# First attention of a fused two-layer kernel: its steps run beside the A projections and half of the output projection

## The chip, the cores and the metric

The kernel runs on one core of one Trainium2 chip. Its metric is the device time of one execution in microseconds (us), compared as the median over several runs.

## The reference, cut to what matters

Two different transformer layers follow each other on a sequence of 512 tokens with 1024 features, all in float32. The change touches the first layer, up to its MLP:

```python
# 512 tokens = 4 tiles of 128 queries; all scores are causal
h = rmsnorm(x, g_pre_mix)
proj = h @ w_in              # q_a k_a v_a | q_i k_i w_i | q_d k_d v_d
# A: 8 heads of 64; each query keeps its 128 best keys, chosen by the indexer
#    sum_h w_i[h] * relu(q_i[h] . k_i)
o_a = softmax(q_a k_a^T / 8, only the kept keys) @ v_a
# D: 4 heads, two maps of 64 each, values 128 wide
o_d = (softmax(q1 k1^T / 8) - lam * softmax(q2 k2^T / 8)) @ v_d
o_d = rmsnorm(o_d) * (1 - lam_init)
x = x + rmsnorm(concat(o_a, o_d) @ w_out, g_post_mix)
x = x + rmsnorm(relu(rmsnorm(x) @ w_up)**2 @ w_down, g_post_mlp)
# then the second layer: windowed attention + mLSTM + a mixture of 32 experts
```

## The kernel before

Every engine has a program of its own, written out by hand in the order in which it runs, and counts semaphores to wait for the others. Tokens lie in 4 tiles of 128 (NT). Eight PSUM banks are handed round.

The projections of the first layer are the list G1 of 30 groups. A group is 8 matmuls in the source, 16 on the engine, of 128x512 with 128 rows. A "rope" group is followed by 4 ScalarE copies of 32 partitions that swap halves (the swaps, L1458) and by 3 VectorE operations (the rope, L1869 to L1871). A "val" group is followed by one ScalarE copy. The order is: 4 groups of q_i, one of k_i, 4 of q_d with a small one for w_i, 4 of k_d, 4 of v_d, and then the A projections, 4 each of q_a, k_a and v_a. Their weights come in chunks through a ring of two slots: a chunk is loaded when the one two before it has been used. Between the groups TensorE runs the indexer's maps (idx_part, L845), three behind each of 8 groups, and VectorE runs the selection of the kept keys (take_steps, 48 passes of MAX8 and MATCH_REPLACE8, L1851 and L1852).

Then comes the attention, alone. It has 48 units: for each query tile i, whose rows are w = 128(i+1) wide, 4 "diff" units (one head of D, two maps) and 8 "topk" units (one head of A, one map), a diff and a topk unit by turns and the last four topk units behind. A unit is: its scores on TensorE (L854), the mask with the row maximum on VectorE (L1927, L1934), the exponential on ScalarE (L1486), for a diff unit the difference of the two maps on VectorE (L1941 to L1945), transposes of 128x128 blocks on TensorE (L865), a copy of them on ScalarE (L1494), and the product with the values on TensorE (L877). TensorE runs the scores of unit a, the transposes of unit a-2 and the values of unit a-3; the scores take turns in 4 banks.

Behind it TensorE turns the mixed output (T_MIX, L786), runs the output projection in 8 groups of the same size (L901, one for each token tile and half of the columns), and turns the normed result (T_MLP) for the MLP, whose up projection starts at L926. Much later the second layer runs a windowed attention in steps of two units (L1134, L1142, L1155), most of them with a dense group (L1065) beside them.

## Time and profile before

| | |
|---|---|
| median of 3 runs | 1961.93 us (1958.96 to 1975.52) |
| profiled execution | 1976.24 us, span 1974.3 us |
| TensorE busy | 1872.6 us, 95% of the span |
| VectorE, ScalarE busy | 780.2 us (40%), 371.1 us (19%) |
| TensorE's share of the chain that ended last | 92% |
| mean granted TensorE clock | 0.945 of full speed |

The granted clock is given as a share of 2.4 GHz; 0.50 is the lower of the two levels, 1.2 GHz. Matmul rows of the profile overlap, since their ends are modelled, so what a group costs is read from the start of its row to the start of the next. An "x16" in a row is 16 instructions on the engine.

### The profile page before, as it was taken

The numbers are of one execution on the slowest core, as the hardware profiler recorded it, in microseconds if no ns is written. First come the engines' busy times: TensorE is split into PE (matmuls) and PEld (weight loads), VectorE is DVE, ScalarE is ACT, GpSimd is POOL, SyncE is SP. The second block draws the span as 40 slices with busy tenths as digits, with TensorE's granted clock in tenths as the row PEclk, the third lists the DMA queues.
The fourth block names the chain that finished last, engine by engine and source line by source line (L and its number), as shares of the span: only waits on it lengthen the run. The fifth ranks groups of instructions, "written<-read, shape, count | busy, mean of one in ns | idle before, by whom it ended". The sixth has DMA issues, their size and how long they took to land.

```text
span 1974.3 us, 24364 instructions
## 1 busy us (share of the span) xinstructions
PE 1872.6 (95%) x9977; PEld 1106.6 (56%) x9977; DVE 780.2 (40%) x1582; ACT 371.1 (19%) x802; POOL 110.4 (6%) x126
## 2 busy tenths in 40 slices
PE   7999999999999999998989989995999999999994
PEld 3344466658888888854556677444444444444441
DVE  3375654445444443525542454233222222222223
ACT  3332254320000000223542231010111111111110
POOL 0000000000000000010003121000000000000001
PEclk9999955999999999998989999995999999999997
DMA  3532200132122222231111112442899999999994
GB/s 120 125 88 85 75 12 1 45 133 84 62 95 92 93 86 86 66 117 43 43 43 43 43 57 85 158 172 78 337 394 384 386 391 391 396 393 395 403 402 168
DMA packets 83826, 329.21 MB, mean 167 GB/s; under 512 B 7895, under 2 KB 9044, under 8 KB 75564
## 3 DMA queue, kind: packets, MB, share of 16 engines
q1 hardware_dynamic: 71964, 287.45, 38.4%
q0 software_dynamic: 7632, 26.11, 4.8%
q10 hardware_dynamic: 4160, 14.68, 1.9%
q8 instruction: 48, 0.79, 0.2%
q14 instruction: 22, 0.18, 0.0%
HBM read 305.41 MB, written 22.81 MB: 166 GB/s over the span
## 4 chain that ended last, share of the span: by engine, by line
PE 92%; DVE 4%; ACT 1%; DMA 1%; issue 1%; POOL 0%; SPq 0%; POOLq 0%; DVEq 0%; ACTq 0%
PE ps L1306 12%; PE ps L926 10%; PE ps L970 10%; PE ps L818 7%; PE ps L1065 6%; PE ps L1314 6%; PE ps L1334 6%; PE ps L901 6%; PE ps L1212 4%; PE ps L1341 3%; PE ps L825 3%; PE ps L1250 3%; PE ps L854 3%; PE ps L877 2%; PE ps L1076 1%; PE ps L1296 1%
## 5 line engine op out<-in xcount | busy, mean ns | idle before, releaser
L1306 PE MATMUL ps<-W,yT 128*64 128x512 f32 x1024 | 229.8, 602 | 1.1 <-DVE yT L2491 1.1
L1306 PEld LDWEIGHTS ps<-W,yT 128*64 128x64 f32 x1024 | 71.3, 138 | 144.4 <-issue 143.0
L818 PE MATMUL ps<-hT,W 128*128 128x512 f32 (+1 forms) x336 | 147.8, 598 | 2.2 <-DVE hT L1784 1.3
L1065 PE MATMUL ps<-hT,W 128*128 128x512 f32 x272 | 126.3, 620 | 0.7 <-ACT gb L1561 0.7
L1314 PE MATMUL ps<-W,yT 128*32 128x256 f32 x2048 | 117.1, 380 | 0.0
L1334 PE MATMUL ps<-W,yT 128*64 128x512 f32 x512 | 116.9, 598 | 0.0
L2517 DVE COPY mix<-ps 32x256 f32<-32x256 f32 x128 | 53.9, 421 | 153.7 <-PE ps L1341 152.5
L818 PEld LDWEIGHTS ps<-hT,W 128*128 128x128 f32 (+1 forms) x336 | 62.8, 189 | 84.7 <-issue 81.4
L1314 PEld LDWEIGHTS ps<-W,yT 128*32 128x32 f32 x2048 | 63.3, 110 | 64.4 <-issue 26.0
L2498 DVE TENSOR_TENSOR yT<-yT,ps 64x512 f32<-64x512 f32 x32 | 22.1, 691 | 191.5 <-ACT yT L1716 191.5
L926 PE MATMUL ps<-yT,cbuf 128*128 128x256 f32 x384 | 87.2, 384 | 2.4 <-issue 2.4
L1065 PEld LDWEIGHTS ps<-hT,W 128*128 128x128 f32 x272 | 53.3, 200 | 63.5 <-issue 62.7
L970 PE MATMUL ps<-cbuf,mix 128*128 128x256 f32 x368 | 81.9, 379 | 0.0
L926 PEld LDWEIGHTS ps<-yT,cbuf 128*128 128x128 f32 x384 | 74.1, 193 | 12.9 <-issue 2.6
L970 PEld LDWEIGHTS ps<-cbuf,mix 128*128 128x128 f32 x368 | 69.9, 190 | 9.5
L1524 ACT ACTIVATE smb<-ps 128x512 f32<-128x512 f32 x10 | 6.0, 595 | 354.2 <-PE ps L970 185.3
L1716 ACT ACTIVATE yT<-ps 64x512 f32<-64x512 f32 x32 | 18.8, 588 | 268.6 <-PE ps L1306 268.6
L1334 PEld LDWEIGHTS ps<-W,yT 128*64 128x64 f32 x512 | 33.9, 136 | 57.0 <-issue 54.8
L1458 ACT ACTIVATE ptb<-ps 32x512 f32<-32x512 f32 x82 | 48.2, 587 | 85.4 <-PE ps L818 84.6
L1341 PE MATMUL ps<-W,yT 128*32 128x256 f32 x1024 | 61.9, 382 | 0.0
L854 PE MATMUL ps<-W 64*128 64x128 f32 (+3 forms) x128 | 60.9, 738 | 0.8 <-issue 0.7
L901 PE MATMUL ps<-W,cbuf 128*128 128x512 f32 x128 | 55.4, 593 | 2.1 <-DVE cbuf L2381 2.1
(400 smaller groups left out, 2709.1 us busy)
## 6 DMA issues: line engine op xcount, KB each, us to landing
W<-in_w_expert_gate SPq DMA_DIRECT2D x32, 2048.0 KB, 16.2
W<-in_w_expert_up SPq DMA_DIRECT2D x32, 2048.0 KB, 21.2
W<-in_w_expert_down SPq DMA_DIRECT2D x32, 2048.0 KB, 21.3
W<-in_w_in SPq DMA_DIRECT2D x16, 2048.0 KB, 7.7
W<-in_w_up SPq DMA_DIRECT2D x8, 2048.0 KB, 8.2
W<-in_w_down SPq DMA_DIRECT2D x8, 2048.0 KB, 7.8
y_scratch<-mix ACTq DMA_DIRECT2D x32, 384.0 KB, 8.9
W<-in_w_out SPq DMA_DIRECT2D x4, 2048.0 KB, 7.8
```

What stands on the lines that cost most here:

```text
L818: ins = pe.matmul(ps[0:n, bank, :], wv[:, k, j * P:j * P + n], hT[:, k, :], start=(k == 0), stop=(k == KT - 1))
L825: ins = pe.matmul(ps[:, bank, :], hT[:, k, j * P:(j + 1) * P], wv[:, k, :], start=(k == 0), stop=(k == KT - 1))
L854: pe.matmul(ps[:, m % 4, 0:un["w"]], q, k, start=True, stop=True).then_inc(score_done, 1)
L901: ins = pe.matmul(ps[:, bank, :], lhs[:, k, i * P:(i + 1) * P], ring_view(c, KT, 512)[:, k, :], start=(k == 0), stop=(k == 7))
L926: ins = pe.matmul(ps[:, bank, 256 * j:256 * j + 256], lhs[:, k, j * P:(j + 1) * P], rhs[:, k, :], start=(j == 0 and k == 0), stop=(j == 1 ...
L970: ins = pe.matmul(ps[:, bank, 256 * t:256 * t + 256], lhs[:, k, t * P:(t + 1) * P], rhs[:, k, :], start=(q == 0 and t == 0 and k == 0), st ...
L1065: ins = pe.matmul(ps[:, bank, :], wv[:, k, j * P:(j + 1) * P], hT[:, k, :], start=(k == 0), stop=(k == KT - 1))
L1212: ins = pe.matmul(ps[:, bank, 256 * j:256 * j + 256], lhs[:, k, j * P:(j + 1) * P], rhs[:, k, :], start=(j == 0 and k == 0), stop=(j == 1 ...
L1306: ins = pe.matmul(ps[64 * part:64 * part + 64, 2, :], xsT[:, x_slot, k, 0:64], wviews[s][part][:, k, :], start=(k == 0), stop=(k == KT - 1))
L1314: ins = pe.matmul(ps[32 * q:32 * q + 32, 3, 0:256], xsT[:, x_slot, k, 64:BLK], wviews[s][q // 2][:, k, 256 * (q % 2):256 * (q % 2) + 256], ...
L1334: ins = pe.matmul(ps[64 * half:64 * half + 64, 4, :], hTa[:, k, :], wviews[s][2][:, k, half * 512:(half + 1) * 512], start=(k == 0), stop= ...
L1341: ins = pe.matmul(ps[32 * q:32 * q + 32, 5, 0:256], hTb[:, k, :], wviews[s][2][:, k, q * 256:(q + 1) * 256], start=(k == 0), stop=(k == 3))
```

## The change

The order of the work in the first layer is written anew. G1 keeps its 30 groups, but only the first 19 run ahead of the attention; the other 11 (three of q_a, four of k_a, four of v_a) run beside it. All 16 diff units now come first, one to a step (steps 0 to 15), then the 32 topk units, two to a step (steps 16 to 31). `group_over(a)` names the group that TensorE runs, whole, at the end of step a: a rope group at steps 0, 2, ..., 12 and a val group at steps 15, 17, 19 and 21. Four of the 8 groups of the output projection follow at steps 23, 25, 28 and 30. In step a TensorE now runs the scores of step a, the transposes of step a-1 and the values of step a-2. The scores have two banks in place of four. ScalarE and VectorE take a group that ran at step a in their step a+1; VectorE does so between the masks and the difference of that step. The weights of q_d are loaded aside at the start, into space that q_a and k_a fill later, and no longer through the ring. The indexer's maps come four behind each of 6 groups. Twelve of the selection's 48 passes move into steps 14 to 25. The banks, turns and loads are renumbered to fit.

```diff
 
+        ASIDE = -1
         G1 = [("rope", 0, c, qiT[:, c, :]) for c in range(4)]
-        G1 += [("ki", 1, 0, kiT), ("rope", 2, 0, qdT[:, 0, :])]
+        G1 += [("ki", 1, 0, kiT), ("rope", ASIDE, 0, qdT[:, 0, :])]
         N_IDX_FROM = len(G1)
-        G1 += [("wi", 2, 0, None)]
-        G1 += [("rope", 2, c, qdT[:, c, :]) for c in range(1, 4)]
-        G1 += [("rope", 3, c, kdT[:, c, :]) for c in range(4)]
-        G1 += [("val", 4, i, vd[:, i, :]) for i in range(NT)]
-        for chunk, dst in ((5, qaT), (6, kaT)):
+        G1 += [("wi", ASIDE, 0, None)]
+        G1 += [("rope", ASIDE, c, qdT[:, c, :]) for c in range(1, 4)]
+        G1 += [("rope", 2, c, kdT[:, c, :]) for c in range(4)]
+        G1 += [("val", 3, i, vd[:, i, :]) for i in range(NT)]
...
+        def group_over(a):
+            if 0 <= a < 14:
+                return None if a % 2 else BESIDE1 + a // 2
+            return BESIDE1 + 7 + (a - 15) // 2 if 15 <= a < 23 and a % 2 else None
...
         def idx_part(g):
 
-            n = 3 * (g - N_IDX_FROM)
-            return list(enumerate(IDX))[n:n + 3] if n >= 0 else []
...
+        STEPS = [[un] for un in units[:len(diffs)]] + [units[u:u + 2] for u in range(len(diffs), N_UNITS1, 2)]
+        N_DIFF, N_STEPS = len(diffs), len(STEPS)
...
-            if n == T_MLP and i == NT - 1:
-                return half
-            return (2 * i + half) % (8 if n == T_MIX else 4)
+            if n in (T_MIX, T_MLP):
+                return 2 + half
+            return (2 * i + half) % 4
+
+        TURNS1 = [(T_MIX, 0), (T_MIX, 1), (T_MIX, 2), (T_MLP, 0), (T_MIX, 3), (T_MLP, 1), (T_MLP, 2), (T_MLP, 3)]
+
+        def turned_by(n, i):
+            if n in (T_MIX, T_MLP):
...
             sp.dma_start(wmask, io["window_mask"]).then_inc(onehot_load, 16)
+            sp.dma_start(qd_w, cols_of(w1, QD, 512)).then_inc(aside_load, 16)
...
+            pe.wait_ge(rope_done, 13)
+            pe.wait_ge(val_done, 4)
+            for a in range(N_STEPS + 2):
+                if a == N_DIFF:
+                    pe.wait_ge(rope_done, 21)
+                if a < N_STEPS:
+                    scores(STEPS[a])
+                if 0 <= a - 1 < N_STEPS:
+                    turn_probs(STEPS[a - 1])
+                if 0 <= a - 2:
+                    values(STEPS[a - 2])
+                if group_over(a):
+                    dense1(group_over(a), (0, 1))
+                if a in (23, 25, 28, 30):
+                    for part in range(2):
+                        out_part(int(a > 27), int(a in (25, 30)), part)
+                if a in (22, 26, 30):
+                    turn(T_MIX, [(a - 22) // 4])
+                if a == 31:
+                    turn(T_MLP, [0])
+            for part in range(2):
+                out_part(2, 0, part)
+            turn(T_MIX, [3])
+            for part in range(2):
+                out_part(2, 1, part)
+            turn(T_MLP, [1])
+            for half in range(2):
+                for part in range(2):
+                    out_part(3, half, part)
...
+            for a in range(N_STEPS + 2):
+                if a < N_STEPS:
+                    exps(STEPS[a])
+                if 0 <= a - 1 < N_STEPS:
+                    take_turned(STEPS[a - 1])
+                if group_over(a - 1):
+                    dense1(group_over(a - 1))
+                if a % 4 == 1 and 5 <= a < 21:
+                    diff_square((a - 5) // 4)
+                if a % 4 == 2 and 6 <= a < 22:
+                    diff_std((a - 6) // 4)
+                if a == 27:
+                    y_norm(0, 0)
+                if a == 28:
+                    norm(T_MLP, 0)
+                if a == 32:
+                    y_norm(0, 1)
+            norm(T_MLP, 1)
+            for i in (2, 3):
                 y_norm(0, i)
                 norm(T_MLP, i)
             def keep(dst, bank, after, n, done):
@@ -1789,7 +1847,7 @@
                 dve.wait_ge(std_done, q + 1)
...
             dve.wait_ge(bline_store, 16)
-            attention(ALL1)
-            for i in range(NT):
-                take_turned(T_MIX, i)
+            for a in range(N_STEPS + 2):
+                if a < N_STEPS:
+                    scores(STEPS[a])
+                if group_over(a - 1):
+                    dense1(group_over(a - 1))
+                if a % 4 == 2 and 6 <= a < 22:
+                    diff_squares((a - 6) // 4)
+                if a % 4 == 3 and 7 <= a < 23:
+                    diff_outputs((a - 7) // 4)
+                if a < N_DIFF:
+                    difference(STEPS[a][0])
+                if a >= 21 and a % 4 == 1:
+                    outputs(STEPS[a - 2][1])
+                if 14 <= a < 26:
+                    next(steps_left, None)
+                if a in (22, 26, 30):
+                    take_turned(T_MIX, (a - 22) // 4)
+                if a == 27:
+                    dve.wait_ge(gb_load, 16)
+                    add_normed(0, T_MLP, 0)
+                if a == 29:
+                    norm_stage(T_MLP, 0)
+                if a == 31:
+                    take_turned(T_MLP, 0)
...
```

TensorE, early steps of the attention. In the names, `W` holds the projected q, k and v (and, with `hT`, the weights of a dense group), `smb` the probabilities, `ptb` the turned probabilities. L854, L865 and L877 before are L906, L917 and L932 now; a dense rope group is L852. Before:

```order
L854 MATMUL ps<-W 128x256 x2
L865 MATMUL ps<-ident,smb 128x128 x2
L877 MATMUL ps<-W,ptb 128x64
L854 MATMUL ps<-W 128x256
L865 MATMUL ps<-ident,smb 128x128 x2
L877 MATMUL ps<-W,ptb 128x128 x2
```

Now, from step 4 to step 6:

```order
L906 MATMUL ps<-W 128x256 x2
L917 MATMUL ps<-ident,smb 128x128
L932 MATMUL ps<-W,ptb 128x128
L852 MATMUL ps<-hT,W 128x512 x8
L906 MATMUL ps<-W 128x256 x2
L917 MATMUL ps<-ident,smb 128x128 x2
L932 MATMUL ps<-W,ptb 128x128
L906 MATMUL ps<-W 128x256 x2
L917 MATMUL ps<-ident,smb 128x128 x2
L932 MATMUL ps<-W,ptb 128x128 x2
L852 MATMUL ps<-hT,W 128x512 x8
```

A dense group of 8 source matmuls now stands behind every second step's values, and the step between has none.

VectorE, from the last mask ahead of a difference on. `ISA` is the mask with the row maximum. Before (the mask of the first topk unit, then the difference of the first diff unit):

```order
L1927 ISA smb,small<-ps,cmask 128x128
L1927 ISA small 128x1
L1934 TENSOR_SCALAR small<-small 128x1
L1941 RECIPROCAL small<-small 128x2
L1942 TENSOR_SCALAR small<-small 128x1
L1944 TENSOR_SCALAR smb<-smb,small 128x128
L1945 SCALAR_TENSOR_TENSOR smb<-smb,small 128x128
```

Now, in step 1, from its second mask on:

```order
L1984 ISA smb,small<-ps,cmask 128x128
L1984 ISA small 128x1
L1987 TENSOR_SCALAR small<-small 128x1
L1927 TENSOR_TENSOR W<-ps,yT 128x512
L1928 TENSOR_TENSOR yT<-yT 128x512
L1929 TENSOR_TENSOR W<-W,yT 128x512
L1994 RECIPROCAL small<-small 128x2
L1995 TENSOR_SCALAR small<-small 128x1
L1997 TENSOR_SCALAR smb<-smb,small 128x128
L1998 SCALAR_TENSOR_TENSOR smb<-smb,small 128x128
```

The three operations of the rope now stand between the masks and the difference of an odd step.

## Rows read from the trace of the kernel before

**Rows 1.** Windows (start:end us; length, busy us and instructions by engine, PEclk, DMA).

```profile
246.00:352.00 106.00, 104.12 (x336) 67.36 (x336) 53.70 (x216) 51.97 (x150) 0.00 (x0) 0.50 0.02 9
352.00:376.00 24.00, 22.92 (x143) 16.08 (x142) 12.42 (x41) 15.04 (x33) 0.00 (x0) 1.00 0.00 1
376.00:437.00 61.00, 61.00 (x186) 30.20 (x185) 23.65 (x33) 9.27 (x19) 0.00 (x0) 1.00 0.29 104
```

**Rows 2.** Timeline of PE in the attention (start us, us, operation, count).

```profile
241.86 1.47 PE L854 MATMUL ps<-W 64*128 64x128 f32 x10 [0.73 <-issue]
...
301.26 0.90 PE L865 MATMUL ps<-ident,smb 128*128 128x128 f32 x3
...
303.37 1.65 PE L854 MATMUL ps<-W 64*128 64x384 f32 x4
...
355.67 1.13 PE L854 MATMUL ps<-W 64*128 64x512 f32 x4
356.73 0.66 PE L865 MATMUL ps<-ident,smb 128*128 128x128 f32 x4
357.22 1.00 PE L877 MATMUL ps<-W,ptb 128*128 128x64 f32 x8
358.15 1.12 PE L854 MATMUL ps<-W 64*128 64x512 f32 x2
```

**Rows 3.** Timeline of DVE and ACT, a diff unit of w = 128, then of 512.

```profile
242.49 0.29 DVE L1927 CUSTOM_DVE_ANT_0 smb<-ps,cmask 128x128 f32<-128x128 f32 x1 [16.34 <-PE ps L854]
...
243.01 0.40 ACT L1486 ACTIVATE smb<-smb,small 128x128 f32<-128x128 f32 x1 [1.25 <-DVE small L1934]
...
244.70 0.35 DVE L1945 SCALAR_TENSOR_TENSOR smb<-smb,small 128x128 f32<-128x128 f32 x1
...
351.45 0.69 DVE L1927 CUSTOM_DVE_ANT_0 smb<-ps,cmask 128x512 f32<-128x512 f32 x1 [1.40 <-PE ps L854]
...
352.38 0.72 ACT L1486 ACTIVATE smb<-smb,small 128x512 f32<-128x512 f32 x1 [3.46 <-DVE small L1934]
...
353.95 0.58 ACT L1494 ACTIVATE ptb<-ps 128x512 f32<-128x512 f32 x1
...
354.88 0.15 DVE L1941 RECIPROCAL small<-small 128x2 f32<-128x2 f32 x1
...
355.84 0.75 DVE L1945 SCALAR_TENSOR_TENSOR smb<-smb,small 128x512 f32<-128x512 f32 x1
```

**Rows 4.** Timeline of ACT and DVE behind a rope group.

```profile
47.94 2.38 ACT L1458 ACTIVATE ptb<-ps 32x512 f32<-32x512 f32 x4 [4.48 <-PE ps L818]
...
50.43 0.69 DVE L1869 TENSOR_TENSOR W<-ps,yT 128x512 f32<-128x512 f32 x1 [4.85 <-ACT ptb L1458]
...
51.76 0.69 DVE L1871 TENSOR_TENSOR W<-W,ptb 128x512 f32<-128x512 f32 x1
```

**Rows 5.** Groups by shape, DVE, 190 to 300 us (busy us, mean ns).

```profile
L1851 DVE MAX8 small<-cbuf 128x8 f32<-128x512 f32 x16 | 11.1, 693 | 0.4
```

**Rows 6.** Timeline of PE in the windowed attention of the second layer.

```profile
949.48 7.08 PE L1065 MATMUL ps<-hT,W 128*128 128x512 f32 x16
...
996.10 0.96 PE L1142 MATMUL ps<-ident,smb 128*128 128x128 f32 x6 [3.01 <-ACT ptb L1623]
...
999.31 9.23 PE L1065 MATMUL ps<-hT,W 128*128 128x512 f32 x16
```

**Rows 7.** Windows of the same attention, columns as in rows 1.

```profile
936.00:940.00 4.00, 3.65 (x30) 2.92 (x28) 3.71 (x10) 2.08 (x9) 0.00 (x0) 1.00 0.00 0
...
997.00:1003.00 6.00, 6.00 (x18) 3.93 (x17) 0.70 (x4) 2.54 (x8) 0.00 (x0) 0.50 0.00 0
```

**Rows 8.** Timeline of PE in the projections.

```profile
55.64 7.13 PE L818 MATMUL ps<-hT,W 128*128 128x512 f32 x16 [0.87 <-DMA W<-in_w_in]
...
77.79 1.13 PE L845 MATMUL ps<-W 64*128 64x256 f32 x6
78.84 7.13 PE L818 MATMUL ps<-hT,W 128*128 128x512 f32 x16
```

More of the change, by code:

```diff
@@ L829, in _ @@
+            for g in range(BESIDE1):
+                if G1[g][0] != "wi":
+                    dense1(g, (0, 1))
+                else:
+                    group(bank1(g), wi_done, 1)
                     pe.wait_ge(swap_done, 5)
                     for i in range(NT):
-                        ins = pe.transpose(ps[:, bank, 8 * i:8 * i + 8], wi_rows[:, i * P:(i + 1) * P], ident[64:72, 64:72])
-                ins.then_inc(proj_done, 1)
+                        ins = pe.transpose(ps[:, bank1(g), 8 * i:8 * i + 8], wi_rows[:, i * P:(i + 1) * P],
+                                           ident[64:72, 64:72])
+                    ins.then_inc(proj_done, 1)
@@ L880, in values @@
                     ins.then_inc(pv_done, 1)
-                for a in range(len(us) + 3):
-                    if a < len(us):
-                        scores(units[us[a]])
-                    if 0 <= a - 2 < len(us):
-                        turn_probs(units[us[a - 2]])
-                    if 0 <= a - 3:
-                        values(units[us[a - 3]])
-            pe.wait_ge(rope_done, 21)
-            pe.wait_ge(val_done, 8)
-            attention(ALL1)
-            turn(T_MIX, [0, 1, 2])
@@ L1258, in _ @@
                 for i in range(NT):
-                    token_group(C_WO2 + half, merged, i, half)
+                    for part in range(2):
+                        token_part(C_WO2 + half, merged, i, 2 * i + half, part)
                     free_when[2 * i + half] = (x_ready, 8 + 4 * half + i + 1)
@@ L1447, in _, with dense1 @@
             act.activation(lamv[:, 2:4], lamv[:, 0:2], ACT.Exp).then_inc(lam_exp, 1)
-            swaps = 0
-            for g, (kind, _, _, dst) in enumerate(G1):
-                bank = 4 + g % 4
+            def dense1(g):
+                kind, _, _, dst = G1[g]
+                bank = bank1(g)
+                swaps = count1(g, ("rope", "ki")) - 1
                 if kind in ("rope", "ki"):
@@ L1467, in _ @@
                     act.activation(dst, ps[:, bank, :], ACT.Copy).then_inc(val_done, 1)
+            for g in range(BESIDE1):
+                dense1(g)
                 if idx_part(g):
@@ L1474, in _, with exps @@
                                        ).then_inc(relu_done, 1)
-            def attention(us):
-                us = list(us)
-                def exps(un):
+            def exps(step):
+                for un in step:
                     for c in range(len(un["maps"])):
@@ L1915, in outputs, with scores @@
                                   ).then_inc(o_evac, 1)
-            def attention(us):
-                us = list(us)
-                def scores(un):
+            def scores(step):
+                for un in step:
                     w = un["w"]
@@ L1962, in attention @@
-                for a in range(len(us) + 7):
-                    if a < len(us):
-                        scores(units[us[a]])
-                    if 0 <= a - 1 < len(us) and units[us[a - 1]]["kind"] == "diff":
-                        difference(units[us[a - 1]])
-                    for lag, kinds, part in ((4, ("topk", "window"), outputs), (5, ("diff",), diff_squares),
-                                             (6, ("diff",), diff_outputs)):
-                        if 0 <= a - lag < len(us) and units[us[a - lag]]["last"] and units[us[a - lag]]["kind"] in kinds:
-                            part(units[us[a - lag]])
@@ L1976, in wide @@
+            assert next(steps_left, "over") == "over"
             def wide(v):
```

335 lines of the change are left out of this document (164 added, 171 removed).

## The prediction

> **What bounds the kernel now.** I read the page first: TensorE is busy for 95% of the span and makes up 92% of the chain that ended last, so a change pays by what it takes off TensorE's path: waits, instructions, or time at the low clock. The windows show where the low clock lies. From 246 to 352 us, in the first attention, the granted clock is 0.50, the level of 1.2 GHz; in the attention's last stretch and in the output projection behind it, it is 1.00 [rows 1]. TensorE fills both, so the attention is bound by TensorE at half speed. It lasts from 241 to 376 us, 135 us.
>
> What it costs at full speed is in the timeline [rows 2]. At w = 512 a unit's scores take 1.06 us from start to start, transposes 0.49, values 0.93. Two maps cost what one costs: x4 is 1.13 us and x2 is 1.12, since the two maps lie on different halves of the rows. At w = 384 and half clock, transposes and values together take 303.37 - 301.26 = 2.11 us, where three quarters of 0.49 + 0.93 is 1.07.
>
> **The change, part by part.** The 11 projection groups, the 8 output groups and the turns are the same before and after, only elsewhere. I therefore price the attention alone, without the dense groups in it, against the 135 us.
>
> Work at full clock. A diff step is scores, transposes and values: 2.5 us at 512, and scaled down with a little fixed cost 1.95, 1.4 and 0.85 for the narrower tiles, four of each: 26.8 us. A topk step is two units that share the time of one score: 1.06 + 2 x 0.49 + 2 x 0.93 = 3.9 at 512, then 3.0, 2.1 and 1.2, four of each: 40.8 us. Together 67.6. If nothing else happened this would be a gain of 67 us.
>
> Waits. The transposes now follow one step behind the scores, not two. In an odd step 1, 3, ..., 13 the difference stands on VectorE behind the rope of the group that TensorE ran just before, and that rope waits for ScalarE's swaps. The chain from the start of the odd step, at w = 128: scores until the first mask 242.49 - 241.86, 0.6 [rows 2, 3]; from there to the end of the second exponential 243.01 + 2 x 0.40 - 242.49 = 1.3 [rows 3]; the copy of the step before, 0.3; swaps 2.4; rope 52.45 - 50.32 = 2.1 [rows 4]; difference until 244.70 + 0.35, 1.2. That is 7.9 us until TensorE can turn the probabilities. At 512: 1.2, then 2.5 (351.45 to 353.95), copy 0.6, swaps 2.4, rope 2.1, difference 1.7 (354.88 to 356.59): 10.5 [rows 3, 4]. Between them I take 8.8 and 9.6. Steps 7 and 11 have VectorE's write of the last tile's outputs in front as well, about 0.9. Sum over the seven odd steps: 2 x 7.9 + 2 x 8.8 + 0.9 + 2 x 9.6 + 0.9 + 10.5 = 64.9. TensorE has for this time only the odd step's scores, the transposes and values of the steps before it, and the next scores, because the dense group of the even step stands behind the transposes that wait: 1.06 + 0.49 + 0.93 + 1.06 = 3.5 at 512 and 2.8, 2.0, 1.2 below, 15.5 in all. So TensorE waits 49.4 us, in seven gaps of some 7 us. This is the largest cost of the change.
>
> Smaller waits. At the start VectorE still has the rope of group 18 and two passes of the selection, each a MAX8 of 0.69 and a replace about as long, 2.9 us in all [rows 5], before its first mask; this shifts the first pair of steps by 2.6. Step 15 waits about 1.0 for the difference of step 14, which has no group beside it. In the topk steps the exponentials are ready after 1.2 + 2.5 us at 512, while TensorE has 3.9 us of other work, so I take 0.3 in five of them, 1.5. Step 28's output group shares its banks with the one of step 23 and waits until VectorE has read them: 3.3, between 0 and a whole group's 7. Waits together: 57.8.
>
> The clock. In the windowed attention the step without a dense group ends in a gap of 3.0 us, and behind it the clock is 0.50 from 997 to 1003; the dense group there takes 9.23 us where its like takes 7.08 [rows 6, 7]. Gaps of 7 us must do the same each time. Seven dense groups then cost 2.15 more each, 15.1. The transposes and values between gap and group double: 0.35, 0.7, 1.05 (2 each) and 1.4, and again 1.4 at step 15: 7.0. Step 28 adds 1.8. Together 23.9.
>
> Sum for the attention: 67.6 + 57.8 + 23.9 = 149.3 us against 135, so **14.3 us more**. The work at half clock is gone, and the waits eat it.
>
> Ahead of it. The weights of q_d are there at once, so the wait of 0.87 for their load goes [rows 8]; the wait for VectorE behind the next group does not, since VectorE's order there is the same. The indexer's maps share their time in pairs too: three maps (x6) cost two turns, 78.84 - 77.79 = 1.05 us at w = 256 [rows 8], and four cost the same. Eight pieces become six; two pieces less at 1.05 to 2.1 each, twice the score of rows 2, are 3.0. VectorE gets more to do there: behind a value group, of 7 us, up to five passes, most at w = 384 and so about 1.2 us each by the 1.46 at 512 [rows 5]. It keeps up. The moved swaps use another buffer and the renumbered banks cost nothing, as each bank's last reader is at least a dense group (7 us) earlier. Part gain: 3.9 us.
>
> Behind it. The last four output groups, the turns and the norms follow as before, each norm chain beside a dense group, and the wait ahead of the MLP's sums stays, since it hangs on the last tile's turn.
>
> Net: 14.3 - 3.9 = **10.4 us slower**. Against the profiled execution of 1976.2 us that is 1986.6; this execution lies 14.3 us above the median of the three runs, so I set the change against the median: 1961.9 + 10.4 = **1972 us**. About 1%, 19.6 us, is what a measurement of this kernel can tell from no change.
>
> **Rivals.** (a) The clock stays at 1.00 through the gaps, because a whole dense group stands on either side of the small work. Then 23.9 us fall away, the attention takes 125.4 us, and the kernel comes out at 1972 - 24 = 1948 us. For it: from 936 to 940, where short steps lie between dense groups, the clock holds at 1.00 [rows 7]. Against it: TensorE is idle there for 0.35 of the 4 us, and the gap of 3.0 us did bring it down [rows 6, 7].
>
> (b) The low clock also holds through the topk part: slower by over 1%. Its place is steps 16 to 31, the nine of them with nothing dense beside them; its price is nine sixteenths of 40.8 us again, 23, and some 4 us for the dense groups that start low: 1972 + 27 = 1999 us. It decides if waits of half a microsecond between small matmuls are enough to bring the clock down. For it: the clock was low through 106 us of the old attention, in which TensorE hardly waited [rows 1]. Against it: 936 to 940 is the same mixture and is at full clock [rows 7]. The Trainium skill, TensorE: Matmul & The Clock Gate, section "A second HAM failure mode: psum-queue depth-cycling", says that frequent micro-idles between groups of matmuls are enough to make the clock swing between its levels. By that rule this rival is the case; the trace agrees for 246 to 352 and disagrees for 936 to 940.
>
> (c) The gaps are shorter than I count, by 3 us each, because swaps and rope begin while the exponentials still run. That is 21 us of waits and part of the clock's cost: 1972 - 27 = 1945 us. Against it: the three engines' orders are fixed and each of these steps waits for the one before.
>
> **How the numbers follow.** Forecast 0.60 (1972; its own range 1958 to 1986, as each gap may be off by 1 us and the smaller waits by as much in sum; of this 0.09 lies beyond 1981.5). Rival (a) 0.12, (b) 0.13, (c) 0.08, and 0.07 for things not seen, spread evenly. Of (a) and (c) together about a third, 0.07, would pass 1% on the fast side, by the scatter of the forecast's own range; with the unseen 0.10. Slower by over 1%: 0.09 + 0.13 + 0.03 = 0.25. Within: 0.65. The range of 1949 to 1993 takes in most of (a) and the near edge of (b).
>
> **What the profile after would show.** TensorE with seven gaps of 6 to 8 us, ended by VectorE's difference, in the diff part; the granted clock at 0.50 behind each and dense groups of some 9 us; next to no gaps and full clock in the topk part, but for one near step 28; the attention with its 11 + 4 dense groups lasting some 149 + 103 = 252 us. I am wrong if the gaps are well below 6 us, if the clock holds through them, or if the topk part is at 0.50.

## The result and the profile after

The changed kernel takes 1984.24 us (median of 4 runs, 1982.50 to 1985.07), against 1960.45 us before. The ratio is 1.0111, with a 95% interval of 1.0074 to 1.0148: slower by 1.1%, 23.8 us, twelve more than the 1972 us that were forecast, and inside the stated range of 1949 to 1993.

The page of the kernel after, with its span, TensorE's busy time, and the granted clock in 40 slices of some 50 us each:

```profile
span 1983.2 us, 24375 instructions
PE 1832.5 (92%) x9977; PEld 1082.4 (55%) x9977; DVE 779.4 (39%) x1582; ACT 379.6 (19%) x808; POOL 110.5 (6%) x126
PEclk9998779999999999998999999995999999999997
```

TensorE is busy for 40 us less than in the first profile of the kernel before, and yet the end comes later: work at half clock has gone, and idle time has come. The windows of the kernel after, in the columns of [rows 1], show the two halves of the new attention, and the stretch of step 28:

```profile
164.00:302.00 138.00, 91.62 (x263) 46.55 (x264) 57.58 (x186) 50.17 (x116) 0.00 (x0) 0.78 0.09 32
302.00:382.00 80.00, 75.03 (x332) 42.36 (x330) 42.45 (x136) 34.36 (x92) 0.00 (x0) 0.99 0.23 79
384.00:388.00 4.00, 4.00 (x6) 1.43 (x5) 0.97 (x4) 3.74 (x9) 0.00 (x0) 0.50 0.00 0
```

In the diff part (164 to 302) TensorE works for only 92 of 138 us, at a mean clock of 0.78. In the topk part it works for 75 of 80 at 0.99. The list of TensorE's waits from 150 to 460 us (total us, times, longest) says what it idles for (without two waits of 0.4 us):

```profile
PE ps L917 <- DVE smb L1998: 46.0, 8, 7.0
PE ps L888 <- DVE x L1881: 3.4, 1, 3.4
PE ps L809 <- ACT ptb L1546: 2.2, 3, 1.0
PE ps L917 <- ACT ptb L1546: 1.2, 3, 0.5
```

L1998 is the last operation of the difference. Of its eight waits one is the start (1.39); the other seven are the odd steps, 44.6 us. The timeline of one of them, step 7, on all three engines, shows the chain that the diff's order fixed:

```profile
228.93 1.27 PE L906 MATMUL ps<-W 64*128 64x384 f32 x4
...
229.45 0.51 ACT L1537 ACTIVATE smb<-smb,small 128x256 f32<-128x256 f32 x1
...
229.96 0.36 ACT L1546 ACTIVATE ptb<-ps 128x256 f32<-128x256 f32 x1
230.35 2.38 ACT L1512 ACTIVATE yT<-ps 32x512 f32<-32x512 f32 x4
232.83 0.69 DVE L1927 TENSOR_TENSOR W<-ps,yT 128x512 f32<-128x512 f32 x1 [3.41 <-ACT yT L1512]
...
234.16 0.69 DVE L1929 TENSOR_TENSOR W<-W,yT 128x512 f32<-128x512 f32 x1
...
234.97 0.69 DVE L2009 TENSOR_TENSOR mix<-ps,small 128x512 f32<-128x512 f32 x1
...
236.41 0.48 DVE L1998 SCALAR_TENSOR_TENSOR smb<-smb,small 128x256 f32<-128x256 f32 x1
...
236.94 0.69 PE L917 MATMUL ps<-ident,smb 128*128 128x128 f32 x2 [6.75 <-DVE smb L1998]
```

Read from top to bottom: TensorE's last work, the second exponential, the copy, the swaps of the dense group, the rope's first and last operation (VectorE waited 3.41 for the swaps), the write of the last tile's outputs, the difference, and then the transposes, after 6.75 us of nothing. The probabilities were ready at 229.96; the difference ended at 236.89. Behind each such gap the clock is low for some microseconds: it is 0.50 from 182 to 186 us, behind the first of them, and 0.87 on average from 186 to 192. Here are steps 2 to 4, TensorE alone; 181.60 is the end of step 1's chain, 199.62 that of step 3's:

```profile
181.60 0.47 PE L917 MATMUL ps<-ident,smb 128*128 128x128 f32 x1 [6.09 <-DVE smb L1998]
...
182.29 9.63 PE L852 MATMUL ps<-hT,W 128*128 128x512 f32 x16
...
192.76 1.12 PE L906 MATMUL ps<-W 64*128 64x256 f32 x4
199.62 0.47 PE L917 MATMUL ps<-ident,smb 128*128 128x128 f32 x1 [5.74 <-DVE smb L1998]
```

A dense group takes 9.63 us behind a gap, where 7.08 is usual [rows 6]. The last costly place is step 28, whose output group waits for its bank and then runs slowly. The start of the MLP is a milestone by which all kernels can be compared: here it is at 448.88 us (before: 436.96, in its first profile).

```profile
383.52 9.77 PE L888 MATMUL ps<-W,hT 128*128 128x512 f32 x16 [3.35 <-DVE x L1881]
...
448.88 1.46 PE L978 MATMUL ps<-hT,W 128*128 128x256 f32 x6
```

So the two profiles differ by 11.9 us at the MLP and by 8.9 in the span, while the medians differ by 23.8. That mismatch is the open question of the result.

### The profile page after: what moved, and what is told of

Read it like the earlier page. It is cut to its first block, busy times and chain, and to the rows that moved or that the text cites. A ratio compares the mean times of both kernels' runs of the same rounds, so it can differ in the third digit from the quotient of the medians.

```text
span 1983.2 us, 24375 instructions
## 1 busy us (share of the span) xinstructions
PE 1832.5 (92%) x9977; PEld 1082.4 (55%) x9977; DVE 779.4 (39%) x1582; ACT 379.6 (19%) x808; POOL 110.5 (6%) x126
## 4 chain that ended last, share of the span: by engine, by line
PE 88%; DVE 5%; ACT 3%; issue 2%; DMA 1%; POOL 0%; POOLq 0%; DVEq 0%; ACTq 0%
PE ps L1359 11%; PE ps L978 10%; PE ps L1022 10%; PE ps L852 8%; PE ps L1117 6%; PE ps L1367 6%; PE ps L1387 6%; PE ps L888 5%; PE ps L1264 4%; PE ps L1394 3%; PE ps L1302 3%; PE ps L848 2%; PE ps L1128 1%; PE ps L1349 1%; ACT yT L1512 1%
## 5 line engine op out<-in xcount | busy, mean ns | idle before, releaser
L852 PE MATMUL ps<-hT,W 128*128 128x512 f32 (+1 forms) x336 | 162.5, 643 | 1.3 <-DVE hT L1842 1.3
L852 PEld LDWEIGHTS ps<-hT,W 128*128 128x128 f32 (+1 forms) x336 | 68.1, 207 | 89.1 <-issue 87.5
L917 PE MATMUL ps<-ident,smb 128*128 128x128 f32 x120 | 22.6, 307 | 47.8 <-DVE smb L1998 46.0
L1537 ACT ACTIVATE smb<-smb,small 128x128 f32<-128x128 f32 (+3 forms) x64 | 35.9, 561 | 149.1 <-DVE small L1987 148.6
L888 PE MATMUL ps<-W,hT 128*128 128x512 f32 x128 | 59.0, 617 | 3.4 <-DVE x L1881 3.4
## 6 DMA issues: line engine op xcount, KB each, us to landing
W<-in_w_expert_gate SPq DMA_DIRECT2D x32, 2048.0 KB, 14.2
```

The source lines that it names most:

```text
L852: ins = pe.matmul(ps[0:n, bank, :], wv[:, k, j * P:j * P + n], hT[:, k, :], start=(k == 0), stop=(k == KT - 1))
L888: ins = pe.matmul(ps[:, bank, :], lhs[:, k, i * P:(i + 1) * P], ring_view(c, KT, 512)[:, k, :], start=(k == 0), stop=(k == 7))
```

## The experiments

The times of the experiments are set against runs of the kernel before on the same chip (medians 1959.4 to 1959.9). The runs that change one thing are edits of the changed kernel, "after" for short. The table gives the start of the MLP in each profile too.

| kernel | median us (range, runs) | ratio to before (95%) | MLP starts at |
|---|---|---|---|
| before, three profiles | 1976.2, 1956.4, 1960.4 | | 436.96, 419.35, 422.08 |
| after, two profiles | 1984.2 (1982.5 to 1985.1, 4); 1983.3 | 1.0111 (1.0074 to 1.0148) | 448.88, 446.12 |
| difference first | 1942.6 (1941.0 to 1943.2, 4) | 0.9909 (0.9890 to 0.9927) | 404.2 |
| dense group ahead | 1939.1 (1937.4 to 1940.2, 4) | 0.9892 (0.9873 to 0.9911) | 402.9 |
| gap filled | 1967.9 (1965.4 to 1969.6, 6) | 1.0037 (1.0019 to 1.0056) | 431.3 |
| swaps first | 1962.7 (1961.4 to 1967.0, 10) | 1.0012 (0.9991 to 1.0034) | 422.2 |
| half groups | 1961.4 (1960.0 to 1963.6, 10) | 1.0006 (0.9987 to 1.0025) | 424.5 |
| output group later | 1981.6 (1978.8 to 1983.8, 4) | 1.0110 (1.0091 to 1.0129) | 448.5 |
| maps by three | 1982.7 (1) | | 448.2 |
| combined | 1932.1 (1930.9 to 1933.6, 4) | 0.9860 (0.9843 to 0.9876) | 396.8 |
| combined, norm later | 1929.4 (1924.5 to 1935.7, 6) | 0.9842 (0.9810 to 0.9874) | 395.5 |

### Difference first: is it the rope that stands in the way?

```diff
 for a in range(N_STEPS + 2):          # VectorE
     if a < N_STEPS:
         scores(STEPS[a])
+    if a < N_DIFF:
+        difference(STEPS[a][0])
     if group_over(a - 1):
         dense1(group_over(a - 1))
...
-    if a < N_DIFF:
-        difference(STEPS[a][0])
```

> The changed kernel with one edit: on VectorE the difference of a step stands ahead of the rope of the dense group beside it, in place of behind it. Theory (the waits come from the order mask, rope, difference, since the rope waits for the swaps): in the changed kernel around 229.96 the second exponential of step 7 has been read, and the difference takes 235.58 to 236.89, so without the rope it would end at about 231.3, where TensorE is free from 230.2 on. The seven gaps shrink from 6.4 us on average to about 1, which takes off 38 us; if the clock then holds through the small work, another 11 us of dense groups at half clock and some 7 of small work go too: about 1928 us, and 1946 if the clock still falls. Rival 1 (the exponentials and masks alone make the wait, the rope only fills it): gaps of 3 us or more are left, 1960 us or above. Rival 2 (the loss lies elsewhere, in VectorE's and ScalarE's sum of work): the waits move behind the rope, to the masks of the next step, and the time stays within 5 us of 1984.

Measured: 1942.6 us, 41.6 less than after. The waits of this kernel, and one of its odd steps, at w = 384:

```profile
PE ps L917 <- DVE smb L1998: 13.0, 9, 1.7
...
PE ps L906 <- DVE small L1984: 2.7, 2, 2.3
```

```profile
221.16 0.61 ACT L1537 ACTIVATE smb<-smb,small 128x384 f32<-128x384 f32 x1
...
222.26 2.39 ACT L1512 ACTIVATE yT<-ps 32x512 f32<-32x512 f32 x4
...
222.80 0.62 DVE L1998 SCALAR_TENSOR_TENSOR smb<-smb,small 128x384 f32<-128x384 f32 x1
223.47 0.55 PE L917 MATMUL ps<-ident,smb 128*128 128x128 f32 x3 [1.57 <-DVE smb L1998]
...
224.53 7.03 PE L852 MATMUL ps<-hT,W 128*128 128x512 f32 x16
```

The difference now ends while the swaps still run, the wait is 1.57 us, and the dense group behind it takes 7.03. The waits for the difference fall by 33.0 us, 2.3 come back as waits of the scores for VectorE's masks, and the remaining 11 of the 41.6 fit the work at half clock that is gone. That lies between the two forecasts for the clock (1928 and 1946): four of the six groups behind a short gap run at full speed, two (8.12 and 8.11 us) do not. Rival 1 (gaps of 3 us or more are left) and rival 2 (no gain) are both out.

### Dense group ahead: the same chain, covered

```diff
 for a in range(N_STEPS + 2):          # TensorE
     ...
+    if group_over(a) and a < N_DIFF:
+        dense1(group_over(a), (0, 1))
     if 0 <= a - 1 < N_STEPS:
         turn_probs(STEPS[a - 1])
     if 0 <= a - 2:
         values(STEPS[a - 2])
-    if group_over(a):
+    if group_over(a) and a >= N_DIFF:
         dense1(group_over(a), (0, 1))
```

> The changed kernel with one edit, on TensorE alone: in the even steps up to 12 the dense group stands ahead of the transposes that wait for the difference, in place of behind the values. VectorE and ScalarE keep their order, rope ahead of difference. Theory: the chain of 8 to 10.5 us stays as long as it was, but a dense group of 7.1 us covers most of it; the next step's masks now stand behind the late difference, so 1 to 2 us are left in each pair: about 35 us less, and with the clock kept up 15 more, 1935 us, or 1950 if the clock still falls. If the waits are no matter of what covers them (rival: VectorE and ScalarE are too full for one step of each pair) the gap comes back one step later and the time stays above 1970.

Measured: 1939.1 us. VectorE and ScalarE still run rope ahead of difference, but TensorE's waits for it are down to 15.2 us:

```profile
PE ps L917 <- DVE smb L2000: 15.2, 10, 5.2
```

The longest, 5.2, is in step 14, where the transposes wait for the difference of step 13 and no dense group stands. (The condition `a < N_DIFF` also moves the value group of step 15 ahead of its transposes.) The waits fall by 30.8 us; the other 14 of the 45.1 us gained fit work at half clock that is gone, since the seven rope groups now take 7.13 each. So the chain costs little where it is covered. It cost 44.6 us because the change put the 7 us of independent work behind the instruction that waits, where an engine that runs in order can't reach them.

### Gap filled: what the clock alone costs

```diff
+    if a in range(2, 16, 2):          # TensorE, ahead of turn_probs
+        g = BESIDE1 + a // 2
+        c, bank = G1[g][1], bank1(g)
+        use_chunk(c)
+        take(bank)
+        for k in range(6):
+            pe.matmul(ps[:, bank, :], ring_view(c, KT, 512)[:, k, 0:P], hT[:, k, :], start=True, stop=True)
```

> The changed kernel, with 6 matmuls more (12 instructions of 512 columns, 5.15 us at full clock, whose result is thrown away) at the place of each of the seven waits, ahead of the transposes that wait. The chains behind the waits are not touched, so TensorE gains no time by it: what the time loses is the price of the clock alone. Theory (each gap brings the clock to 0.50 for the work behind it): the dense groups go back from 8.2 to 9.6 us to 7.1, 11 us in sum over the six that were read, and the transposes, values and scores behind the gaps lose about 1 us each, 18 us less in all: 1966 us. Rival (the clock falls for another reason than the idle time, such as the small matmuls): it stays at 0.50 in these places and the time is that of the changed kernel or, by the filler at half clock running over the end of the wait, 10 to 25 us more.

Measured: 1967.9 us, 16.3 less than after, although the kernel does seven times 12 matmul instructions more. The filler is L950:

```profile
237.23 1.42 PE L906 MATMUL ps<-W 64*128 64x384 f32 x4
238.58 5.42 PE L950 MATMUL ps<-hT,W 128*128 128x512 f32 x12
245.01 0.55 PE L917 MATMUL ps<-ident,smb 128*128 128x128 f32 x3 [1.02 <-DVE smb L2005]
...
246.07 7.03 PE L852 MATMUL ps<-hT,W 128*128 128x512 f32 x16
```

From the scores at 237.23 to the transposes at 245.01 it takes 7.8 us; in after the same two instructions start at 248.93 and 256.71, 7.8 us too. The chain is the same, and behind it the dense group costs 7.03 and not 9. Six of the seven chains agree in this way within 0.02 us. The first filler starts at half clock, takes 7.12 us and ends 0.8 us too late, and step 15 now waits 1.64 us that it didn't wait before; in the stage alone, from the first scores to those of step 16, this kernel takes 133.1 us and the second profile of after 147.3, which is 14.2 less. So the clock behind the seven gaps is worth 14 to 17 us (14.2, or 16.7 with the 0.8 and the 1.64). The small matmuls alone don't bring it down, since they are all still there. The filler adds dense work as well as taking the idle time away; the kernel with the difference first, which adds no work, points the same way.

### Swaps first: another link of the chain

```diff
     if a < N_STEPS:                   # ScalarE
+        if group_over(a - 1) and a < N_DIFF:
+            dense1(group_over(a - 1))
         exps(STEPS[a])
     if 0 <= a - 1 < N_STEPS:
         take_turned(STEPS[a - 1])
-    if group_over(a - 1):
+    if group_over(a - 1) and a >= N_DIFF:
         dense1(group_over(a - 1))
```

> The changed kernel with one edit, on ScalarE alone: in the odd steps up to 13 the four swaps of the dense group stand ahead of the step's exponentials, in place of behind them and the copy. Theory (a chain of exponentials, copy, swaps, rope, difference ends each gap): the swaps of 2.4 us now begin with the step, the rope ends some 4.6 us after it, and the exponentials at 3.8 to 5, so that the difference is there after 5.8 to 6.4 us in place of 7.9 to 10.5. Each gap shrinks by 2 to 4 us, 20 in sum, and a gap of some 3.5 us still brings the clock down: 1964 us. Rival (the wait hangs on VectorE's own work, not on ScalarE's order): less than 5 us of change.

Measured: 1962.7 us, 21.5 less. The waits for the difference add up to 26.5 us in place of 46.0; the dense group behind one of them:

```profile
222.53 0.69 PE L917 MATMUL ps<-ident,smb 128*128 128x128 f32 x2 [3.99 <-DVE smb L2000]
...
223.86 9.04 PE L852 MATMUL ps<-hT,W 128*128 128x512 f32 x16
```

All six dense groups behind such gaps (2.90 to 3.99 us) take 8.07 to 9.05. A gap of 3 to 4 us brought the clock down here just as one of 6 to 7 did, so this edit gets the waits' share back, 19.5 us, and next to nothing of the clock's.

### Half groups: how much work stands ahead of the wait

```diff
 def group_over(a):
     if 0 <= a < 14:
-        return None if a % 2 else BESIDE1 + a // 2
+        return BESIDE1 + a // 2 if a % 2 else None
...
-    if group_over(a):                 # TensorE
+    if 0 <= a < 14:
+        dense1(BESIDE1 + a // 2, (a % 2,))
+    elif group_over(a):
         dense1(group_over(a), (0, 1))
```

> The changed kernel with one edit: each of the seven rope groups beside the diff units is run in two halves, one at the end of the even step and one at the end of the odd step behind it, in place of whole in the even step. VectorE and ScalarE keep their orders and take the group in the step after its second half, rope ahead of difference, so the same chain of 8 to 10.5 us stands there. Theory (what counts is how much of TensorE's work stands between the scores and the transposes of the step that holds the chain): it is now the small work of 1.2 to 3.5 us and half a group, 3.5 us, so 3 us are left of each gap: about 24 us less, and if gaps of 3 us still bring the clock down, no more: 1960 us; 1945 if it holds. Rival (the gap follows from a whole group standing at once, since it starves the other engines for 7 us): the waits vanish and it comes out as the difference moved ahead did, 1940.

Measured: 1961.4 us. With 3.5 us more of work inside the chain six of the gaps are 2.9 to 3.8 us, and the seventh chain, now in step 14 where there is no group at all, makes a gap of 7.15:

```profile
214.67 0.69 PE L917 MATMUL ps<-ident,smb 128*128 128x128 f32 x2 [3.67 <-DVE smb L2000]
...
216.01 4.37 PE L852 MATMUL ps<-hT,W 128*128 128x512 f32 x8
```

Five of the six halves behind the shorter gaps cost 4.4 to 5.3 us in place of 3.5; the sixth, behind a gap of 3.44, takes 3.60. The rival, by which the waits vanish, is out. Spreading the dense work evenly is not what helps; what stands between the scores and the transposes that wait is.

### Output group later: the bank of step 28

```diff
-    if a in (23, 25, 28, 30):
+    if a in (23, 25, 29, 31):
         for part in range(2):
-            out_part(int(a > 27), int(a in (25, 30)), part)
+            out_part(int(a > 27), int(a in (25, 31)), part)
```

> The changed kernel with one edit, on TensorE alone: the two output groups of steps 28 and 30 stand in steps 29 and 31. In the changed kernel the one of step 28 waits 3.35 us for its bank (the norm of the first tile's output has still to read it) and then takes 9.77 us in place of 7.08. Theory: one step of two topk units takes 3.9 us, which covers the 3.35, and with the wait the fall of the clock goes: 6 us less, 1978. Rival: the wait is only moved to the next transposes or to the turn of the first normed tile behind step 31: 1984, no change.

Measured: 1981.6 us, 2.6 less, within the scatter of both (their ranges overlap). The wait for the bank is gone and another stands in its place, 3.88 us long:

```profile
383.16 2.92 PE L906 MATMUL ps<-W 64*128 64x512 f32 x4 [3.88 <-DVE small L1984]
```

The scores wait for masks, and these stand on VectorE behind the same add (L1881) that the output group waited for, which in turn stood 4.21 us behind ScalarE's square root. The rival is right, in a form that it didn't name: the late thing is the norm, not the bank.

### Maps by three: the part ahead

```diff
-            n = 4 * (g - N_IDX_FROM)
-            return list(enumerate(IDX))[n:n + 4] if n >= 0 else []
+            n = 3 * (g - N_IDX_FROM)
+            return list(enumerate(IDX))[n:n + 3] if n >= 0 else []
```

> The changed kernel with one edit: the indexer's maps come three behind each of 8 groups again, in place of four behind each of 6. Looked at is the start of the first scores, which lies between 161.2 and 162.5 us in four kernels whose part ahead of the attention is the changed one. Theory (maps share their time in pairs, so three cost as much as four): two pieces more cost 3.0 us and the first scores start at 164.3 to 165. Rival (a map costs its own time): the start stays within 0.5 us.

Measured in the profile: the first scores start at 164.66 us, 2.7 later than in the second profile of after (161.92), as the theory has it. Its time, 1982.7 in one run, does not show these 2.7 us: they are 2.1 at the MLP and gone by the end, which is the size of what single runs differ by.

### The two kernels once more

> The kernel before, unchanged, profiled a second time. Its profiled execution took 1976.2 us at a mean granted clock of 0.945; its other runs lie between 1955 and 1967 with the clock between 0.951 and 0.960, so they spend less time at half clock. Theory: the difference lies in the first attention, where the clock was 0.50 from 246 to 352 us; in a run of 1958 us this stretch holds some 15 us less, and the attention lasts about 120 us in place of 135. Rival: the attention lasts 135 us in this run too, and the 15 us lie in other stages at half clock (the start of the projections, the second layer). If this run is again at 1976, the two traces should agree within 2 us stage by stage and the question stays open.

> The kernel before, unchanged, profiled a third time. In the first profile the first attention lasted 134 us, with the clock at 0.50 for 106 us in a row; in the second 116 us, with the clock going up and down. Theory (the time of a run of this kernel follows from how long the first attention stays at half clock, and nothing else moves by more than 3 us): whatever this run takes, the distance of its span from 1954.4 us equals the distance of its attention from 116 us within 3 us. Rival: the distance lies in the second layer.

> The changed kernel, unchanged, profiled a second time. In its first profile a stretch at half clock at the start of the projections (20 to 24 us) cost 1.5 us or more, which four kernels with the same part ahead did not have. Theory (that stretch is chance): this run shows 1.00 there and starts its first scores near 161.5 us in place of 164.2; the seven gaps sum to 44.6 us again within 0.5, since nothing in them depends on chance. Rival: the stretch belongs to the changed kernel and is there again.

The second profile of before took 1956.4 us. Its first scores start at 242.43 and the turns behind the attention at 358.29, so its attention lasts 115.9 us, where the first profile has 134.0 (241.86, [rows 2], to 375.90) and the third, at 1960.4 us, 242.25 to 361.01, 118.8. Windows of the second profile, then two lines of its timeline:

```profile
246.00:280.00 34.00, 31.71 (x114) 21.22 (x113) 21.31 (x105) 19.83 (x71) 0.00 (x0) 0.55 0.08 31
280.00:290.00 10.00, 8.86 (x48) 5.50 (x46) 6.55 (x26) 7.55 (x20) 0.00 (x0) 1.00 0.00 0
290.00:310.00 20.00, 18.40 (x78) 11.67 (x79) 12.71 (x46) 10.69 (x32) 0.00 (x0) 0.74 0.00 1
310.00:322.00 12.00, 10.53 (x60) 6.74 (x59) 6.61 (x24) 9.10 (x20) 0.00 (x0) 1.00 0.01 2
```

```profile
291.26 1.06 PE L877 MATMUL ps<-W,ptb 128*128 128x64 f32 x4 [2.41 <-ACT ptb L1494]
...
322.52 1.54 PE L877 MATMUL ps<-W,ptb 128*128 128x64 f32 x6 [2.00 <-ACT ptb L1494]
```

In this run the old attention, from 280 us on, is at full clock, but for the stretches behind the waits of 2.41 and 2.00 us. In the first profile it stayed at 0.50 until 352 [rows 1]. Both spans and attentions agree: third against second profile, 4.2 us of span and 2.9 of attention; first against second, 19.9 and 18.2. So what makes these three runs of the kernel before differ is, for the most part, how long its first attention stays at half clock. The other runs have no profile, but agree: over 15 of them on one chip the time falls, by and large, as the mean granted clock of the whole run rises, from 1976.7 us at 0.944 over 1966.9 at 0.951 to 1955.2 at 0.960. (That mean doesn't say in which stage the clock was low.) The changed kernel's four runs differ by less than 3 us.

The second profile of after bears out its expectation: first scores at 161.92, the clock at 1.00 from 20 to 24 us (0.57 in the first profile), and 46.0 us of waits for the difference again, to the tenth.

### Combined

Four edits: the difference first, every dense group ahead of the transposes, the value groups at even steps, and the output groups later. The third is new, and the second now takes in the value groups of the topk steps:

```diff
-            return BESIDE1 + 7 + (a - 15) // 2 if 15 <= a < 23 and a % 2 else None
+            return BESIDE1 + 7 + (a - 14) // 2 if 14 <= a < 22 and a % 2 == 0 else None
```

> The changed kernel with four edits: the difference ahead of the rope on VectorE; every dense group ahead of the transposes on TensorE; the four value groups at steps 14, 16, 18 and 20 in place of 15, 17, 19 and 21; the output groups of steps 28 and 30 at 29 and 31. From the dense group moved alone (1939.1 us): of the 15.2 us that its transposes still wait for differences 12 go, the 5.2 of step 15 among them; the bank's wait at step 28 and its half clock, 6. Theory: 1921 us. Rival (the waits of about 1.4 us that are left in both single edits come from something that both leave in place, the exponentials): each edit gives nothing beyond the other, and it is 1934.

Measured: 1932.1 us, 11 more than the theory. The waits of this kernel:

```profile
PE ps L906 <- DVE small L1984: 5.6, 4, 3.9
PE ps L917 <- DVE smb L1998: 4.5, 3, 1.6
PE ps L809 <- ACT ptb L1546: 3.2, 3, 1.9
```

The waits for the difference fell from 15.2 to 4.5, close to the 12 expected, so the rival's reason (a shared remainder of exponentials) is wrong although its number is nearer. The largest part of what is missing, 6 us by the expectation, is step 28, where the 3.9 us stayed as in the kernel with the output group later, with half clock behind it. A smaller one is step 16, where the scores wait 1.06 and 0.31 us for masks and the value group behind them takes 8.83; the rest was not followed up. The chain at step 28, in this kernel:

```profile
321.72 1.02 ACT L1471 ACTIVATE yT<-ps 128x1024 f32<-128x1024 f32 x1
...
322.85 1.28 ACT L1492 ACT_TABLE_LOAD   x1
324.15 0.29 ACT L1492 ACTIVATE small<-small 128x1 f32<-128x1 f32 x1
...
324.54 0.16 DVE L1873 RECIPROCAL small<-small 128x1 f32<-128x1 f32 x1 [4.21 <-ACT small L1492]
...
326.06 1.23 DVE L1881 TENSOR_TENSOR x<-x,stage 128x1024 f32<-128x1024 f32 x1
...
327.95 2.92 PE L906 MATMUL ps<-W 64*128 64x512 f32 x4 [3.88 <-DVE small L1984]
```

The last run takes the add out of VectorE's way:

```diff
-                if a == 28:           # ScalarE
+                if a == 29:
                     norm(T_MLP, 0)
...
-                if a == 27:           # VectorE
+                if a == 28:
                     dve.wait_ge(gb_load, 16)
                     add_normed(0, T_MLP, 0)
-                if a == 29:
+                if a == 30:
                     norm_stage(T_MLP, 0)
```

> The combined kernel, with the add of the first tile's normed output one step later on VectorE (28 in place of 27), and the norm behind it one step later on ScalarE and VectorE (29 and 30). In the combined kernel VectorE stands from 320.3 to 324.5 at step 27 behind the square root that ScalarE starts only after the step's exponentials and copies, and the masks of step 28 stand behind it, so that the scores wait 3.88 us at 327.95 and then run at half clock. Theory: one step later the square root is there, the add takes 2.7 us beside the work of step 28, the 3.9 us of wait go and with them about 3 us of half clock: 1925 us. Rival (VectorE's 2.7 us of add and 2.4 of masks, with ScalarE's two table loads of 1.28, fill the step anyway): 1930 or more.

Measured: 1929.4 us, with runs from 1924.5 to 1935.7, which doesn't separate it from 1932.1. The 3.88 us are gone, and 2.66 of them are back on another engine:

```profile
326.28 1.28 ACT L1537 ACT_TABLE_LOAD   x1
...
329.00 0.84 ACT L1546 ACTIVATE ptb<-ps 128x384 f32<-128x384 f32 x2
...
329.61 1.94 PE L917 MATMUL ps<-ident,smb 128*128 128x128 f32 x8 [2.66 <-ACT ptb L1546]
```

The square root costs ScalarE two table loads (`ACT_TABLE_LOAD`) of 1.28 us here, one for it and one back to the exponential, and now the copies that TensorE needs stand behind them. The Trainium skill, ScalarE: Activation LUTs, section "What ACT_TABLE_LOAD costs", gives about 1283 ns for the load, which the rows bear out, and a drain of about 1380 ns beside it, which they don't: in the rows of the combined kernel the load stands 0.1 us behind the sum of squares, and the square root 0.02 us behind the load. Either kernel beats both originals: 1.4 to 1.6% faster than before, and 2.6 to 2.8% faster than the change as it was made.

## Why the prediction was right, and where it was off

**The mechanism** held as written: seven gaps that VectorE's difference ends, half clock behind each, next to no wait in the topk part, and one wait at step 28. Moving the difference, covering the chain, and moving the swaps each took away about what this chain predicts: 41.6, 45.1 and 21.5 us, where 38 to 56, 35 to 50 and 20 were expected.

**The gaps.** Forecast 49.4 us, measured 44.6. The chains were sized well: in step 7 the scores start at 227.48 and the transposes at 236.94, 9.5 us against 8.8 + 0.9; at w = 384 (step 9) it is 247.15 to 256.71, 9.6 against 9.6. But TensorE's own work beside them is longer than counted, 2.7 us in step 7 (227.48 to 230.20) where I took 2.0, so that what the waits lack is work. Waits together: 57.8 forecast, 46.0 + 7.6 = 53.6 measured (the 7.6 are, but for 0.4 at step 1, the waits of the topk part: its step 28 has 3.35 against 3.3 forecast, and three of 0.5 to 0.95 us are ahead of turns, where I forecast none).

**The clock.** Forecast 23.9, measured 16.3 (gap filled, by the medians) and 2.7 at step 28 (9.77 against 7.08), 19.0 in all. The count was wrong: I charged seven dense groups behind a gap, but behind the gap of step 13 stands step 14, which has none. The size was high as well. In the second profile of after, the six groups take 9.38, 9.03, 8.09, 8.91, 8.96 and 8.58, 1.7 more than 7.08 on average and not 2.15.

**The small work.** The 67.6 us for it were some 6 low: of the 146.4 us worked out below, 73.8 remain without the waits and the clock. The 252 us for the length of the new attention also left out the four turns beside the topk steps (4.2 us). In the second profile of after, the attention runs from 161.92 to the output group behind its last step at 415.98, 254.1 us where 252 were forecast. Without 15 dense groups at 6.9 each from start to start and without the turns it is 146.4; the forecast had 149.3. That the sum came so near is in part luck: the waits and the clock were 4 and 5 us too high, the small work 6 too low.

**Ahead of it.** Forecast -3.9. The 19th group of G1, the last that both kernels run ahead, starts at 158.96 us in the third profile of before and at 154.96 in the second of after: -4.0. The first profiles of both differ by only 1.3 (158.56 and 157.25); the changed kernel had a stretch at a low clock there, from 20 to 24 us, that its second profile doesn't have.

**The step that failed** is the base: "this execution lies 14.3 us above the median of the three runs, so I set the change against the median". I priced the new attention against the 135 us of the profiled execution and then took the result from the median of other executions, as if their attention lasted 135 us too. It lasts 116 to 119. Those 14.3 us lay in the very stage that the change replaces (its attention was 15.3 us longer in the first profile than in the third, at 1960.4 us), and the new attention doesn't have this wandering stretch. With 118.8 in place of 135, the same sum is 149.3 - 118.8 - 3.9 = +26.6, 1988.5 us; with the terms as measured, 146.4 - 118.8 - 4.0 = +23.6, against 23.8 of the medians and 24.0 at the start of the MLP between the third profile of before and the second of after. The forecast of +10.4 was close to the difference of the two first profiles at the MLP, 11.9. That the range held is partly luck: the time lies at the slow end of the forecast's own 1958 to 1986, and the edge of 1993 had been set by rival (b), which is not what happened.

**The rivals.** (a) The clock stays up: out, with dense groups of 8.1 to 9.6 us behind the gaps. (b) Low clock through the topk part: out, 0.99 there, with waits of 0.4 to 1.0 us among small matmuls. The rule of the Trainium skill behind it (TensorE: Matmul & The Clock Gate, section "A second HAM failure mode: psum-queue depth-cycling") is not borne out by waits of that length here. The second profile of before speaks against the reading of the old attention on which I rested this rival: the same small matmuls ran at 1.00 there from 280 to 290 us, and the falls came behind waits of 2.41 and 2.00. (c) Shorter gaps: out for the order as made; 4.8 us in sum, not 21.

That the old attention stays at 0.50 for over 100 us in one run and for half of that in another is shown; what lets it return in one and not in the other was not tried and stays open.

## What to carry to other kernels

Where independent work is put beside a chain, ask on which side of the waiting instruction it stands: with the seven dense groups of 7 us behind the transposes the kernel was 1.1% slower than before, with the same groups ahead of them 1.1% faster. Order each engine's own list so that the operation that TensorE waits for comes ahead of work that nobody waits for: a move of one line on VectorE was worth 42 us.

When a profiled execution is slower than the other runs, find out in which stage before setting a change against their median. A stage at half clock that the change replaces is the first suspect, the mean granted clock of each run hints at it, and one more profile tells it.

## What the runs showed of the hardware

- The same kernel stayed at half clock for different lengths of time in different executions: the same program had 0.50 in its first attention for 106 us in one profile and for about 52 and 64 in the two others (worked out from a mean of 0.77 over 112 us and of 0.72 over 115), and its attention lasted 134.0, 115.9 and 118.8 us.
- Gaps of 2.9 to 4.0 us brought the clock down nearly as surely as gaps of 5.7 to 7.0: the dense group behind one took 9.04 us with a gap of 3.99 and 8.95 with one of 6.75. Of twelve such shorter gaps (swaps first, half groups) eleven had slow dense work behind them; the one of 3.44 us had not. Gaps of 1.2 to 1.6 us in the kernel with the difference first mostly did not (7.03), but twice did in part (8.12 and 8.11).
- Discarded matmuls in a gap paid for themselves: 84 instructions more, 16.3 us less (gap filled).
